# Ranking 24 of 32 experts by token count on the chip, and letting the eight smallest share units two by two

## What is computed

```python
def reference(...):
    u = rmsnorm(h, g_mix);  z = u @ w_in
    h = h + concat([pool_mixer(z[..., :512]), ssm_mixer(z[..., 512:])]) @ w_out
    h = h + hierarchical_moe(rmsnorm(h, g_ffn), ...)
    gate = sigmoid(rmsnorm(h, g_ple) @ ple_gate_w + ple_gate_b)
    h = h + gate * (p @ ple_proj_w)
    return rmsnorm(h, g_final)

def hierarchical_moe(v, ...):       # 4 groups of 8 experts, 32 experts in all
    # top-1 group of each token, then the top-2 experts within it, weights renormalised
    for g in range(4):
        hg = silu(einsum('td,edf->tef', t, w_gate[g])) * einsum('td,edf->tef', t, w_up[g])
        hg = hg * combine[:, g, :, None]
        out = out + einsum('tef,efd->td', hg, w_down[g])
```

## Time and profile before

| | us |
|---|---|
| median of three runs | 513.37 |
| the profiled execution, its own time | 511.78 |
| its span, first to last instruction | 509.9 |
| TensorE busy | 472.7 (93%) |
| VectorE, ScalarE, GpSimd busy | 231.9, 169.8, 150.0 |
| granted TensorE clock, mean | 0.994 |

### The profile page before, as it was taken

The page is one execution under the profiler, slowest core; times in us unless marked ns, Lnnn a source line. Parts: engine busy times, 40 slices in busy tenths (PEclk is TensorE's granted clock), DMA queues, the critical chain, the costliest instruction groups (busy, mean ns, idle before and its releaser), DMA issues.

```text
span 509.9 us, 9824 instructions
## 1 busy us (share of the span) xinstructions
PE 472.7 (93%) x3998; PEld 252.7 (50%) x3998; DVE 231.9 (45%) x683; ACT 169.8 (33%) x283; POOL 150.0 (29%) x136
## 2 busy tenths in 40 slices
PE   3799999999999999999999999977999897999993
PEld 3345555744854467655555544433444443444441
DVE  2899949999233248652222222211111111466525
ACT  6633576647442333121111111121212111214454
POOL 1079999714100001232222222211210210004250
PEclk9999999999999999999999999999999999999997
DMA  8874200399499976899999999999999996990022
GB/s 300 151 205 91 65 0 2 134 151 178 158 353 412 421 331 222 315 395 422 417 417 418 418 415 410 419 420 417 420 421 417 416 408 276 372 409 7 0 82 82
DMA packets 60149, 144.90 MB, mean 284 GB/s; under 512 B 27586, under 2 KB 36838, under 8 KB 47816
## 3 DMA queue, kind: packets, MB, share of 16 engines
q1 hardware_dynamic: 54504, 133.92, 71.3%
q0 software_dynamic: 5328, 10.31, 5.3%
q10 hardware_dynamic: 272, 0.04, 0.0%
HBM read 138.17 MB, written 14.19 MB: 299 GB/s over the span
## 4 chain that ended last, share of the span: by engine, by line
PE 63%; DMA 22%; SPq 6%; DVE 4%; issue 2%; ACT 2%; POOL 0%; DVEq 0%; POOLq 0%
PE bank L1654 58%; DMA big<-in_exp_w_up_dram 6%; DMA ring<-in_exp_w_up_dram 6%; DMA h<-in_exp_w_up_dram 6%; DMA moe<-v_d,gidx_all 4%; SPq L389 3%; SPq L365 2%; PE bank L2060 1%; PE bank L1754 1%; PE bank L1744 1%; DVE moe L923 1%; PE bank L1917 1%; ACT moe L551 1%; PE bank L2180 1%; PE bank L2080 1%
## 5 line engine op out<-in xcount | busy, mean ns | idle before, releaser
L1654 PE MATMUL bank<-ring,moe 128*32 128x256 f32 (+2 forms) x1568 | 109.0, 411 | 6.2 <-DMA ring<-in_exp_w_up_dram 5.4
L1580 POOL DMA_INDIRECT pairs_d<-moe,sidx_all x32 | 31.8, 994 | 155.2 <-PE bank L2060 77.0
L1654 PEld LDWEIGHTS bank<-ring,moe 128*32 128x32 f32 (+1 forms) x1568 | 53.9, 112 | 46.4 <-issue 13.9
L923 DVE TENSOR_TENSOR vrow<-moe,bank 64x128 f32<-64x128 f32 x64 | 18.6, 291 | 118.2 <-ACT moe L822 117.2
L1654 PE MATMUL bank<-ut,big 128*128 128x512 f32 x128 | 57.7, 597 | 1.9 <-ACT ut L563 1.9
L822 ACT ACTIVATE moe<-bank 64x256 f32<-64x256 f32 x32 | 12.1, 377 | 136.8 <-PE bank L1654 136.8
L551 ACT ACTIVATE moe<-bank 128x512 f32<-128x512 f32 (+1 forms) x65 | 36.5, 582 | 60.6 <-PE bank L1654 50.5
L1654 PE MATMUL bank<-ring,ut 128*128 128x512 f32 x128 | 55.7, 593 | 0.4 <-DVE ut L923 0.4
L1654 PE MATMUL bank<-big,moe 128*32 128x256 f32 (+1 forms) x528 | 41.7, 426 | 3.6 <-DMA big<-in_exp_w_up_dram 2.4
L923 DVE TENSOR_TENSOR ring<-ring,bank 128x64 f32<-128x64 f32 (+1 forms) x142 | 39.3, 277 | 2.8
L1654 PEld LDWEIGHTS bank<-ring,ut 128*128 128x128 f32 x128 | 24.0, 190 | 29.3 <-issue 29.3
(11 more groups left out here) (198 smaller groups left out, 611.8 us busy)
## 6 DMA issues: line engine op xcount, KB each, us to landing
ring<-in_exp_w_gate_dram SPq DMA_DIRECT2D x19, 1024.0 KB, 24.5
ring<-in_exp_w_down_dram SPq DMA_DIRECT2D x18, 1024.0 KB, 29.3
ring<-in_exp_w_up_dram SPq DMA_DIRECT2D x17, 1024.0 KB, 26.1
big<-in_exp_w_up_dram SPq DMA_DIRECT2D x7, 1024.0 KB, 17.1
big<-in_exp_w_down_dram SPq DMA_DIRECT2D x7, 1024.0 KB, 24.4
big<-in_exp_w_gate_dram SPq DMA_DIRECT2D x6, 1024.0 KB, 17.9
ut<-in_exp_w_up_dram SPq DMA_DIRECT2D x4, 1024.0 KB, 24.9
h<-in_exp_w_down_dram SPq DMA_DIRECT2D x4, 1024.0 KB, 19.0
```

Source lines behind the costliest of these rows:

```text
L923: return dve.tensor_tensor(o, a, b, op)
L1580: pool.indirect_dma_start(pairs, bass.IndirectOffsetOnAxis(ap=index, axis=0), at(moe, ALL, M_Y + k * 512, [[1, 512]]), None, bounds_check= ...
L1654: return pe.matmul(o, a, b, start=start, stop=stop, skip_group_check=loose)
```

## The change

There are now 28 units where there were 32 experts. Units 0 to 7 are experts 0 to 7 as before. Units 8 to 23 are the sixteen experts with most tokens among experts 8 to 31, and units 24 to 27 hold the eight with fewest, two to a unit: one has the first 32 rows of the unit's 64, the other the last 32. A unit of two needs six pieces of weights, so there are still 96 pieces. Its matmuls are as many as those of a unit of one, with each row half going to its own expert's weights.

- **Ranking.** TensorE sums each expert's count to its own partition (`counted`, after `rank(1)` and ahead of `picked(2)`). VectorE builds keys, compares, sums and makes a one-hot of the positions. TensorE (`sorted_rows`, behind `gu_step(0)`) turns that into the list of experts by rank and turns the table; VectorE writes `order_i` (`order`). TensorE permutes the table (`permuted`, behind `gu_step(1)`), and VectorE makes the indices of units 8 to 27 after the second hidden product.
- **Loading.** SyncE waits for the list (`sort_sb` at LISTED) ahead of piece 23, the first of unit 8, and reads each expert's number from `order_i` into a register; the address of its pieces comes from it.
- **Spread.** Units 26 and 27 are the ones that `combined` serves. The one-hot matrices for it come from a small table in HBM (`aux_d`, one store and two gathers by GpSimd) and eight VectorE operations in step 20 (`spread`). The old building, its eight transposes (`slots`) and its copies are gone.
- **Loads behind the experts.** All four row tiles `h` are issued first, then the first 1 MB of gate weights, then pairs 0, the other gate 1 MB, pairs 1, the bias, pairs 2, the second gate half (2 MB), pairs 3. The buffers of the pairs, gates and sigmoids move.
- `P_PROJ` is (21, 23, 25, 26) for (21, 23, 25, 27), and its matmuls stand ahead of `gu_step`.
- **Overflow** now runs all 8 rounds when some count is over 64 or the largest of the eight smallest is over 32. By the reference's inputs that one is 30.

```diff
+FIRST, HIGH, LOW = 8, 16, 8
+NU = FIRST + HIGH + LOW // 2
+SORTED = HIGH + LOW
...
+        def members(u):
+
+            return 2 if u >= FIRST + HIGH else 1
+
+        def early_pieces(u):
+
+            return [(u, k, i) for k in (0, 1) for i in range(members(u))]
+
+        def late_pieces(u):
+
+            return [(u, 2, i) for i in range(members(u))]
+
+        ORDER = early_pieces(0) + [x for u in range(NU - 1) for x in early_pieces(u + 1) + late_pieces(u)] + late_pieces(NU - 1)
...
+            e = u if u < FIRST else sorted_at(u - FIRST if u < FIRST + HIGH else 2 * (u - FIRST) - HIGH + n)
+            load_piece(eng, e, k, to, gu_ready[u % LOADS] if k < 2 else down_ready[u % LOADS])
...
+            def sorted_at(r):
+
+                if not at_rank:
+                    sp.wait_ge(sort_sb, LISTED)
+                if r not in at_rank:
+                    at_rank[r] = sp.value_load(at(order_i, (0, 1), r, [[1, 1]]), min_val=0, max_val=NE - 1)
+                return at_rank[r]
...
-            sp.wait_ge(gu_ps, NE - 5)
-            sp.wait_ge(dn_ps, NE - 6)
-            load_h(0)
-            sp.wait_ge(gu_ps, NE - 1)
+            sp.wait_ge(gu_ps, NU - 2)
+            sp.wait_ge(dn_ps, NU - 3)
+            for t in range(NT):
+                load_h(t)
+            sp.wait_ge(gu_ps, NU - 1)
             load_gate(0, 0, 4, ld_wple)
+            sp.wait_ge(dn_ps, NU - 2)
             sp.wait_ge(moe_done, 1)
-            sp.wait_ge(gu_ps, NE)
             load_pairs(0)
-            sp.wait_ge(dn_ps, NE - 1)
             load_gate(0, 4, 4, ld_wple)
-            load_h(1)
             load_pairs(1)
-            load_gate(1, 0, KC, ld_wple1)
             sp.dma_start(at(moe, ALL, M_BP, [[1, DM]]),
                          dr(A["ple_gate_b"], 0, [[0, P], [1, DM]])).then_inc(ld_bias, 16)
-            load_h(2)
+            sp.wait_ge(dn_ps, NU - 1)
             load_pairs(2)
-            load_h(3)
-            sp.wait_ge(dn_ps, NE)
+            sp.wait_ge(gu_ps, NU)
+            load_gate(1, 0, KC, ld_wple1)
             load_pairs(3)
...
+            def counted():
+
+                for t in range(NT):
+                    got = mm(bank[7][0:NE, 0:1], at(moe, ALL, Q["MS"] + t * NE, [[1, NE]]), at(cst, ALL, C_ONE, [[1, 1]]),
+                             t == 0, t == NT - 1)
+                got.then_inc(sort_ps, 1)
+
+            def sorted_rows():
+
+                pe.wait_ge(sort_sb, HOT)
+                hot = at(rw, (0, NE), RW_HOT, [[1, SORTED]])
+                mm(bank[7][0:1, 0:SORTED], at(cst, (0, NE), C_PAIR, [[1, 1]]), hot, True, True)
+                mm(bank[7][0:1, NE:NE + SORTED], at(rw, (0, NE), RW_NUM, [[1, 1]]), hot, True, True)
+                pe.transpose(bank[7][0:NE, P:2 * P], at(rw, ALL, RW_TF, [[1, NE]]), ident).then_inc(sort_ps, 1)
...
+            def order():
+
+                dve.wait_ge(sort_ps, ORDERED)
+                dve.tensor_scalar(at(order_i, (0, 1), 0, [[1, SORTED]]), at(bank[7], (0, 1), 0, [[1, SORTED]]), 0.5, None,
+                                  ALU.mult).then_inc(sort_sb, 1)
...
+            def permuted():
+
+                dve.wait_ge(sort_ps, PERMUTED)
+                seq(dve.tensor_scalar(at(tblw, ALL, FIRST, [[1, NU - FIRST]]), bank[7][:, 0:NU - FIRST], float(EMPTY), 0.0,
+                                      ALU.add, ALU.max))
+                indices(FIRST, NU - FIRST)
...
-                        for lo in range(0, CAP, HALF):
-                            last = mm(bank[dst][n * CAP + lo:n * CAP + lo + HALF, 0:DE],
-                                      at(moe, ALL, M_XT + k * DM + j * P + odd * CAP + lo, [[1, HALF]]),
+                    for n, both in enumerate((gate_w, up_w)):
+                        for i, w in enumerate(both):
+                            lo = n * CAP + i * HALF
+                            last = mm(bank[dst][lo:lo + HALF, 0:DE],
+                                      at(moe, ALL, M_XT + k * DM + j * P + odd * CAP + i * HALF, [[1, HALF]]),
                                       at(w[0], ALL, w[1] + j * DE, [[1, DE]]), j == 0, j == KC - 1)
...
             gu_step(0, table)
+            sorted_rows()
             h_step(0)
             gu_step(1)
+            permuted()
             down_step(0)
-            slots(NE - 1)
-            slots(NE - 2)
```

More of the change, by code:

```diff
@@ L321, in build, with place, landed, pairs_at @@
                 AFTER.append(q)
-        def place(e, k):
-            i = SPOT[ORDER.index((e, k))]
-            return ((ring, i * PIECE) if i < 12 else (big, (i - 12) * PIECE) if i < 16 else
-                    (zbuf, (i - 16) * PIECE) if i < 18 else (h, (i - 18) * PIECE) if i < 20 else (ut, (i - 20) * PIECE))
-        E_RN, E_SG, E_O = 2 * PIECE, 4 * PIECE, 2 * PIECE
+        def place(u, k):
+            found = []
+            for n in range(members(u)):
+                i = SPOT[ORDER.index((u, k, n))]
+                found.append((ring, i * PIECE) if i < 12 else (big, (i - 12) * PIECE) if i < 16 else
+                             (zbuf, (i - 16) * PIECE) if i < 18 else (h, (i - 18) * PIECE) if i < 20 else (ut, (i - 20) * PIECE))
+            return (found * 2)[:2]
+        def landed(u, per):
+            return 16 * per * sum(members(v) for v in range(u % LOADS, u + 1, LOADS))
+        E_RN, E_SG, E_O = 2 * PIECE, 2 * PIECE, 2 * PIECE
         E_PPW, E_PIN, E_PPT = 10 * PIECE, 11 * PIECE, 11 * PIECE + NT * DPLE
         NA = NT - 1
-        E_WPLE = (8 * PIECE, 0)
-        O_SLOT, O_Y = 3 * PIECE, (NE - 3) % YBUF
+        E_WPLE = (0, 8 * PIECE)
+        O_SLOT, O_Y = 3 * PIECE, (NU - 3) % YBUF
         E_S = E_PIN
         M_GF, M_BP = 4096, 5120
+        def pairs_at(t):
+            return (ring, (4 + t) * PIECE) if t < 2 else (big, (t - 2) * PIECE)
+        def spread_at(i, t, parts):
+            return (at(ring, parts, E_S + t * P, [[1, P]]) if i else
+                    at(small, parts, S_S30 + t * P, [[1, P]]) if t < 2 else at(rw, parts, (t - 2) * P, [[1, P]]))
         def stores(e):
@@ L846, in _ @@
             silu(0)
-            for e in range(NE):
-                if e + 1 < NE:
+            for e in range(NU):
+                if e in P_PROJ:
+                    for n in range(2):
+                        pp_out(2 * P_PROJ.index(e) + n)
+                if e + 1 < NU:
                     silu(e + 1)
@@ L851, in _ @@
                     p_rows_out()
-                if e in P_PROJ:
-                    for n in range(2):
-                        pp_out(2 * P_PROJ.index(e) + n)
                 if e == 0:
-                    slots_30_out()
                     act.wait_ge(slot_done, 1)
@@ L1341, in step @@
                 if e == 0:
+                    order()
                     weights_and_slots()
@@ L2010, in _ @@
             rank(1)
+            counted()
             picked(2)
@@ L2131, in _ @@
                     x_step(e // 2 + 1)
-                if e + 1 < NE:
+                if e in P_PROJ:
+                    if e - 1 in P_PROJ:
+                        pe.wait_ge(pp_done, 2 * P_PROJ.index(e - 1) + 2)
+                    for n in range(2):
+                        proj(e, 2 * P_PROJ.index(e) + n)
+                if e + 1 < NU:
                     gu_step(e + 1)
@@ L2135, in _ @@
                     p_rows()
-                if e in P_PROJ:
-                    for n in range(2):
-                        proj(e, 2 * P_PROJ.index(e) + n)
                 down_step(e)
```

311 lines of the change are left out of this document (178 added, 133 removed).

## The result

| | before | after |
|---|---|---|
| median of the runs, us | 513.37 | 518.2 |
| the profiled execution, its own time | 511.78 | 518.2 |
| its span | 509.9 | 516.5 |
| TensorE busy | 472.7 | 461.3 |
| granted TensorE clock, mean | 0.994 | 0.961 |

The ratio is 1.0092 (95% interval 1.007 to 1.0115): the changed kernel is slower by 4.8 us, against a forecast of 5.5. The spans differ by 6.6 us. The profiled execution of before lay 1.6 under its median and that of after on it, which accounts for most of the rest.

A forecast was written before the change was run, and what follows sets the result against it. Weight loading by DMA, not TensorE, was taken as the bound. Profiled 511.78 + 2.0 (start) + 3.5 (behind the weights) = 517.3 us, as a median 513.37 + 5.5 = 518.9 us; 8-in-10 range 512.0 to 525.0.

The forecast's parts named there:

- What bounds the kernel: In the experts: weight loading is the slower side, so removing 24 us of TensorE work gains 0.
- The start of the experts, +2.0: Before the first paired-scheme unit: ranking and the wait for the list leave a lasting DMA hole, 2.0 us (1.2 to 4).
- SyncE in the steady state, 0: Weight issues of 24 experts: a register load each stays under 1 us a piece where 2.5 are allowed, 0 us.
- Rival 4: SyncE's weight issues: register addresses make SyncE the bound, 3 us an issue adding 36 us, 550 us; chance 0.07.
- Behind the weights, +3.5: After the last weights: loads queued ahead delay pairs 0 and the second gate half, 3.3 plus 0.2, 3.5 us.
- W: End of the experts: the moment the last weights land, put at about 431.5 us before the change.
- the rule weighed there: SyncE's queue behind the experts: skill says completion needn't follow ring order; forecast took landings in issue order, pairs 0 3.5 us later.
- rival 3: Gaps before the last units: TensorE's clock still low at the last down and combining, 5 us more, 523.9 us; chance 0.14.
- step 4: Loads behind the last weights: the new queue order makes TensorE wait for pairs 0, 3.5 us more in all.
- Rival 1: Loads behind the last weights: their order does no harm, only the early hole counts, 514.3 us; chance 0.22.
- Rival 2: Gathers and scatters of every unit: cost by call, 0.6 us each, six fewer give 3.7 us, 510.6 us; chance 0.11.
- Rival 5: Overflow branch: its loop runs and costs hundreds of us; chance 0.01.

The follow-up runs named there:

- the second kernel: The changed kernel with the old order of loads plus four idle matmuls ahead of the weight waits of units 24 to 27: 517.59 us, ratio 1.0045.

## Why the prediction was right, and where not

1. **What bounds the kernel.** Right. The DMA share from 260 to 420 us is 1.01 to 1.02 in after while TensorE's busy time falls; 44 us less of arithmetic changed nothing, and with half the bytes the four units were worth 24.9 us. The gain of 24 us that was put at 0 was 0 within what the runs can tell.
2. **The start of the experts, +2.0.** This is the term that was mis-sized. The last weights landed 0.80 later than before (432.69 against 431.89; forecast 2.0), the gates began 0.7 to 1.1 later in the two exchanges of the order, and the medians show nothing (1.0005 with the old order). Even these do not come from the ranking: after's profile is 0.76 behind at VectorE's first reciprocal of the norm that feeds the router (175.58 against 174.82), where none of the ranking has run. The other profiles with the old head have 174.75 to 175.10 there, those with the changed one 175.10 to 175.82; why is open. From that point to the last weights it takes 257.1 us in before and in after alike, and 257.2 to 257.5 in the other profiles of the changed kernel with whole pieces, but for the one with fixed experts, which has 258.4. Of the parts, `counted` was put at 1.2 us and took 0.41; its matmuls have one column where those of `rank` have 32. The rank matmuls came 0.84 later (203.47 against 202.63), nearly all of it those 0.76. Together piece 22 went 1.36 later (214.15), near the 1.2 of the sum but for other reasons, which is luck. The list was written at 215.97 (forecast 216.0) and piece 23 went at 217.07, so semaphore and register took 1.1 us where 1.4 were allowed. The step that failed is the last one, that this wait makes a hole that stays. Piece 23 landed at 222.65 (forecast 222.1) with the wait and at 222.71 without it. I had priced the loss by the soonest of all landings and taken for granted that piece 23 could have landed much sooner when it was issued sooner; issued 2.9 us sooner, it took 8.5 us to land and not 5.6.
3. **SyncE in the steady state, 0.** Right. Issues whose address comes from a register took 0.33 to 0.42 us while the queue had room, the same as others. Rival 4 falls.
4. **Behind the weights, +3.5.** Right in mechanism and size. From W to the start of the gates it took 16.06 us for 12.10, so 4.0 more, and 3.5 without the 0.5 of the slow turning. Pairs 0 landed at W + 10.15 (forecast 10.0), tile 0 was turned from W + 14.1 (13.8), the gates began at W + 16.1 (15.8), and the second gate half landed at W + 24.3 (23.8), just in time for its matmuls at 458.46. The order alone, exchanged in both directions, moves the start of the gates by 3.6 and 4.1 us. Said wrong on the side were before's W, 431.89 where I had 431.5, and that `combined` could start 1 us sooner: it began at 435.50 against 435.32, and was not the last wait.
   On the rule weighed there: in after, pairs 0 and the loads issued behind them landed at 442.84, 445.52, 448.05, 449.33, 451.80, 456.95 and 459.41, in the order of their issue. The Trainium skill (DMA: Bandwidth & Descriptors, Queues, rings and completion order) allows completion out of order; the trace shows none for these whole loads. It can't tell for the row tiles: rows and pairs of a tile raise one semaphore, and in the run with the old order, for instance, the 439.66 that the profile gives as the landing of tile 1's rows is only the 16th of the 32 counts that the two loads raise together. For a budget of several MB the order of issue is what counted here.
5. **The clock.** I had seen that it may fall and put it in rival 3, at the wrong place. In the gaps before the last units it did fall (0.81 and 0.83 from 380 to 420 us), where it costs nothing, as the rival said. But the prediction looked for its price at W, in the last down and in `combined`, which took in after what they took before; in the profiles with fixed experts and with the longer combining the last down did take 3.55 and 3.62 us for 1.93, but `combined` no more than before, and with fixed experts the wait for pairs 0 took this up. The price in after came behind them, at the wait of 4.05 us that step 4 itself makes: 1.9 us in the first gate group, and 0.9 in the turning, of which 0.5 shows in the start of the gates. The sum contained this gap, and its length could have been worked out: tile 0's turning at W + 13.8 less the end of `combined` at W + 10 to W + 11, so 2.8 to 3.8 us, between the 2.96 that kept the clock and the 4 that lost it. The Trainium skill (TensorE: Matmul & The Clock Gate, HAM oscillation — how this bites in real kernels) tells of a kernel in which each wait for a DMA lowers the clock anew. Here the trace agrees for the wait of 4.05 us, and not for every wait: the clock stayed at 1.00 behind 2.37 and 2.96 us in the kernel before.
6. **The sum.** 2.0 + 3.5 = 5.5 was forecast; the medians say 4.8 and the spans 6.6, with before's profile 1.6 under its median. The spans divide into 0.8 by which the last weights came later (forecast 2.0), 3.5 for the order (3.5) and 0.5 + 1.9 for the clock (0). So two errors nearly cancel: the start was at least 1 us too dear, and the clock's 2.4 were missing. That the sum came so near is in part luck; the term of the order, which carries the loss, is not. Order and clock go together: with the old order nothing of the loss is left.
7. **The rivals.** Rival 1 (the order does no harm) falls with the two exchanges. Rival 2 (0.6 us for a call) falls with 24 calls that cost 0.2 to 1.7 us in all, as far as calls without rows can tell; its six calls fewer are four, with the two gathers from `aux_d`. Rival 3 is right as to the fall, and in after wrong as to place and price. Rival 5, the overflow, did not run: the executions lie within 2 us of each other.

## What to carry to other kernels

- Where two engines both look full, ask what each would do if the other had less work. Here a stretch with a DMA share of 1.02 beside a TensorE with gaps told the bound, and 24 us of arithmetic were worth nothing until the bytes were halved.
- A queue that lands in order is a plan, if the trace shows that it does. To fill a hole in it with loads that are wanted later delays the one that is wanted first, by their transfer time: add up the megabytes in front of the first load that someone waits for.
- When a sum contains a new wait of TensorE as long as one behind which the clock fell in some trace at hand, price the clock behind it too (here 2.4 us), and put work into the gap if there is any that can be done early.
- Before a later start is put down to a change, look how late the run already is at a point ahead of the changed work. Here that was 0.76 us of the 0.80 by which the last weights came later.

## What the runs showed beside this

- **A standstill at a jump.** TensorE stood still for 5.12 and 5.27 us where it reads a flag and jumps over a branch that is not taken, in the profiles of two of the kernels; in neither the profile of before nor that of after. Eight of twelve executions of the second kernel took about as long as the profiled one. Its cause stays open.
- **The last gap alone does not tell whether the clock holds.** The 80 matmuls of the last expert's gate and up took 5.38 us behind a gap of 2.37 in the kernel before and 6.92 behind one of 2.40 with the added calls. The last down, 16 matmuls, took 3.62 us behind a gap of 2.78 in the kernel with the longer combining, and 1.92 behind one of 2.82 in the last kernel, whose clock had been held by idle matmuls through the units before. A gap of 2.96 between full experts left it at 1.00 too, and in the kernel with fixed experts it fell at one of 2.47. Something beside the length of the gap decides; no run here tells what.
- **Calls of indirect transfers whose rows are all dropped** still bring 80 packets each, cost the other transfers 0.1 us each at most, and GpSimd 0.98.
- **The 16 parts of a load land far apart when the queue is long.** Each load raises its semaphore 16 times. For the piece issued at 398.20 in the kernel before, the trace has the first of these at 413.7 and the last at 429.0, so W is the time of the part that comes last. With the short queue behind the weights the 16 of pairs 0 lie between 437.3 and 438.0.
